# Block products for the last six contraction tiles of a fused decoder layer's first down projection

## What is computed

```python
x = x + 0.5 * swiglu(rmsnorm(x, ffn1_norm), w_gate, w_up, w_down)   # first block, hidden width 2816
u = rmsnorm(x, mix_norm)
proj = u @ w_in                     # convolutions, RG-LRU scan, SSD scan follow
x = x + concat(lru_out, ssd_out) @ w_out
x = x + 0.5 * swiglu(rmsnorm(x, ffn2_norm), ...)                    # second block, same shapes
y = rmsnorm(x, final_norm)
```

## Time and profile before

| | us |
|---|---|
| median of 3 runs (lowest, highest) | 2099.49 (2099.32, 2099.60) |
| the profiled execution | 2098.3 |
| its span, first to last instruction | 2096.6 |
| TensorE busy | 2082.2 |
| DVE busy | 1473.5 |
| POOL busy | 950.2 |
| ACT busy | 865.9 |
| DMA, mean over the span | 109 GB/s |

### The profile page before, as it was taken

One profiled execution on the slowest core, in us unless ns is written; L12 is line 12 of the kernel. 1 busy time (PEld: TensorE's weight loads), 2 busy tenths in 40 slices (PEclk: granted clock), 3 DMA queues, 4 the chain that ended last, 5 costly groups with the idle time before them and its releaser, 6 DMA issues.

```text
span 2096.6 us, 37492 instructions
## 1 busy us (share of the span) xinstructions
PE 2082.2 (99%) x15762; PEld 2051.4 (98%) x15762; DVE 1473.5 (70%) x1361; ACT 865.9 (41%) x1288; POOL 950.2 (45%) x580
## 2 busy tenths in 40 slices
PE   9999999999999999999999999999999999999998
PEld 9999999999999999999999999999999999999998
DVE  7878667676644568878788596786766766675546
ACT  7433333352422235678786540124333333352324
POOL 4644445456643222352534552324544444464650
PEclk9999999999999999999999999999999999999999
DMA  5133232363523322310112422131223222456132
GB/s 174 62 122 122 82 121 102 142 223 122 182 84 106 115 81 101 123 54 32 54 43 75 149 81 94 48 125 61 108 95 109 110 106 88 176 182 226 58 122 81
DMA packets 83383, 227.48 MB, mean 109 GB/s; under 512 B 9608, under 2 KB 18312, under 8 KB 83216
## 3 DMA queue, kind: packets, MB, share of 16 engines
q1 hardware_dynamic: 82064, 224.56, 30.1%
q10 hardware_dynamic: 1152, 0.52, 0.1%
HBM read 162.05 MB, written 63.17 MB: 107 GB/s over the span
## 4 chain that ended last, share of the span: by engine, by line
PE 92%; DVE 3%; ACT 2%; DVEq 1%; issue 1%; DMA 0%; ACTq 0%; POOL 0%; SPq 0%; POOLq 0%
PE banks L997 54%; PE banks L867 28%; PE banks L911 3%; PE banks L1267 2%; PE banks L1178 0%; ACT gate_a L1543 0%; PE banks L1025 0%; PE banks L1032 0%; PE banks L1038 0%; PE banks L1174 0%; PE banks L1156 0%; ACT gate_x L1543 0%; PE banks L1148 0%; DVE decay L2213 0%; DVEq L2178 0%
## 5 line engine op out<-in xcount | busy, mean ns | idle before, releaser
L867 PE MATMUL banks<-u_hi,w_lo 128*128 128x344 f32 x864 | 285.8, 331 | 0.6 <-DVE lru_even L1748 0.3
L867 PE MATMUL banks<-u_hi,w_hi 128*128 128x344 f32 x864 | 275.9, 319 | 0.0
L867 PE MATMUL banks<-u_lo,w_hi 128*128 128x344 f32 x864 | 275.7, 319 | 0.0
L740 POOL TENSOR_TENSOR w_lo<-w_raw,w_hi 128x1024 fp32r<-128x1024 f32 (+1 forms) x68 | 167.1, 2457 | 166.4 <-DVE xbc L2184 123.6
L738 POOL TENSOR_SCALAR w_hi<-w_raw 128x1024 fp32r<-128x1024 f32 (+1 forms) x59 | 67.4, 1142 | 342.3 <-PE banks L867 274.6
L867 PEld LDWEIGHTS banks<-u_hi,w_lo 128*128 128x128 f32 x864 | 162.4, 188 | 7.4 <-issue 4.9
L867 PEld LDWEIGHTS banks<-u_hi,w_hi 128*128 128x128 f32 x864 | 162.4, 188 | 5.1 <-issue 4.3
L867 PEld LDWEIGHTS banks<-u_lo,w_hi 128*128 128x128 f32 x864 | 162.4, 188 | 0.0
L997 PE MATMUL banks<-mix_hi,w_lo 128*128 128x258 f32 x864 | 158.1, 283 | 0.0
L997 PE MATMUL banks<-mix_hi,w_hi 128*128 128x258 f32 x864 | 157.9, 283 | 0.0
L997 PE MATMUL banks<-mix_hi,w 128*128 128x258 f32 x832 | 151.5, 283 | 0.0
(11 more groups left out here) (374 smaller groups left out, 6677.3 us busy)
## 6 DMA issues: line engine op xcount, KB each, us to landing
w_raw<-in_gate_up SPq DMA_DIRECT2D x46, 512.0 KB, 4.1
hidden<-up SPq DMA_DIRECT2D x44, 516.0 KB, 3.6
raw<-in_gate_up SPq DMA_DIRECT2D x40, 512.0 KB, 4.1
w_raw<-in_w_in SPq DMA_DIRECT2D x36, 512.0 KB, 4.1
hidden_mix<-hidden_part SPq DMA_DIRECT2D x16, 1032.0 KB, 4.8
slot_raw<-hidden_mix SPq DMA_DIRECT2D x16, 1032.0 KB, 5.8
slot_raw<-hidden SPq DMA_DIRECT2D x12, 1032.0 KB, 6.8
raw<-in_down SPq DMA_DIRECT2D x16, 512.0 KB, 4.6
```

The costliest lines, as they stand in the source:

```text
L740: pool.tensor_tensor(w_lo[s][:, 0:n], w_raw[s][:, 0:n], w_hi[s][:, 0:n].bitcast(F32), ALU.subtract).then_inc(split, 1)
L867: end = pe.matmul(out[:, c, 0:CH], w[s][:, k * P:(k + 1) * P], x[kx][:, c * CH:(c + 1) * CH], start=(first and n == 0), stop=(last and n = ...
```

## The change

In the first block only, the down groups go on over the six tiles left: `NL` = 28 takes the place of the old count and `NE` = 32 is the new one, with `LAST_K` = 3 contraction tiles in each block of groups 28 to 31, so that a product there is 3 x 2 x 3 = 18 matmuls. The units d1 are gone. Hidden pairs 0, 9 and 10 get mixes too; pair 0 is read back from DRAM for it. Seven *end slots* of 3x516 columns are loaded, and their parts made, at the end of group 27 and in group 28. The preparation of u (high, square, low, total) is put between the products of groups 29 to 31, the rest of it after group 31, and `sums("mix")` stands after the seventh contraction tile of xbc 0. In both blocks `slot_low` of slots 1 to 3 stands one product earlier in group 19, and slot 7 later.

The core of the change, from the file's diff:

```diff
+def depth(q):
+    return 4 if q < NL else LAST_K
...
             def store_hidden(f, i):
...
+            def store_mix(f, n):
+                sp.wait_ge(*f.h_mixed.past(n + 1))
+                sp.dma_start(d.hidden_mix[:, n], f.part_end if n == FT // 2 - 1 else f.part).then_inc(f.mix_stored.sem, 16)
...
             def down(f, x_src, src):
-                tag = f.tag
+                if f is f1:
+                    store_mix(f, MIXED)
                 load_slot(f, 0)
                 for m in range(2):
                     x_again(f, x_src, m)
                 store_hidden(f, NG // 2 - 1)
+                if f is f1:
+                    store_mix(f, MIXED + 1)
                 for m in range(2, 4):
                     x_again(f, x_src, m)
                 down_weights(f, src, NG)
                 for o in range(1, 5):
                     load_slot(f, o)
...
-                    for k in range(4):
+                    for k in range(depth(q)):
...
-                hooks = {0: {6: lambda: sums("mix", m1.tot, KT - 1)}, 3: {3: dt_turn}, 4: {6: bc_turn}, 5: {5: dt_widen}}.get(q)
+                hooks = {0: {7: mix_sums}, 3: {3: dt_turn}, 4: {6: bc_turn}, 5: {5: dt_widen}}.get(q)
...
                 if o == 0:
-                    act.wait_ge(*f.mix_stored.past(16 * MIXED))
+                    act.wait_ge(*f.mix_stored.past(16 * (MIXED + 2 * (f is f1))))
...
+            next_after = {number(NL + 1, "p2"): lambda: two_next(0), number(NL + 2, "p2"): lambda: two_next(2),
+                          number(NE - 1, "p5"): lambda: (next_high(4), next_square(4))}
...
                         if q // 2 <= MIXED:
-                            hidden_mixes(f, q // 2)
+                            hidden_mixes(f, q // 2 - 1, f.u, f.part)
+                        elif f is f1:
+                            hidden_mixes(f, q // 2, f.u, f.part)
...
                     if q == NG - 1:
-                        between = {"p2": lambda: slot_low(f, 0), "p5": lambda: weight_sums(f, NG), "p7": lambda: slot_low(f, 1),
-                                   "p3": lambda: slot_low(f, 2)}
+                        between = {"p2": lambda: slot_low(f, 0), "p5": lambda: (weight_sums(f, NG), slot_low(f, 1)),
+                                   "p7": lambda: slot_low(f, 2), "p3": lambda: slot_low(f, 3)}
                     corners(f, q, between)
                 last_corner(f, NG - 1)
-                slot_low(f, 3)
...
+                def last_product():
+                    product(f, NG // 2, 1)
+                    if f is f1:
+                        dve.drain()
+                        hidden_mixes(f, f.mixes - 1, f.u, f.part_end)
...
+                    hooks.update({NL - 2: {"p6": lambda: slot_low(f, 14)},
+                                  NL - 1: {"p5": lambda: slot_low(f, 15), "p7": lambda: (slot_low(f, 16), weight_sums(f, NL)),
+                                           "p3": lambda: slot_low(f, 17)},
+                                  NL: {"p1": lambda: slot_low(f, 18), "p6": lambda: slot_low(f, 19), "p5": lambda: slot_low(f, 20)},
+                                  NL + 1: {"p5": lambda: next_low(0), "p3": lambda: next_low(1), "p4": lambda: add("mix", 1, m1)},
+                                  NL + 2: {"p5": lambda: next_low(2), "p3": lambda: next_low(3), "p4": lambda: add("mix", 2, m1)},
+                                  NE - 1: {"p1": lambda: add("mix", 3, m1), "p7": lambda: next_low(4),
+                                           "p3": lambda: add("mix", 4, m1)}})
```

More of the change, by code:

```diff
@@ L156, in make_plan @@
             p.unit(("u" + tag, j), gate_up[2 * j + 1], KT)
[L157 to L166, removed]
+    for m in range(KT):
+        p.unit(("d2", m), d.down2[m, :, 8 * BLOCKS * P:], N_LAST)
+    s = 1
     for q in range(XT):
@@ L196, in make_plan @@
     p.before_ffn2 = list(p.taken)
-    ffn("2", 0)
+    s = 0
+    for m in range(WHOLE):
+        p.take(("d2", m), s)
+        s = 1 - s
     return p
@@ L569, in gate_up_groups @@
                         store_hidden(f, q // 2 - 1)
+                        if q > 2:
+                            store_mix(f, q // 2 - 2)
+                    if f is f1 and q == NG - 4:
+                        sp.wait_ge(*f.h_stored.past(32))
+                        for m in range(2):
+                            sp.dma_start(f.again[m], d.hidden[:, 2 * pair_place(0) + m, :]).then_inc(x_landed[m], 16)
             def x_again(f, src, m):
@@ L1234, in tensor @@
             ffn(f2)
+            for m in range(WHOLE):
+                banks_read(f2, ("d2", m))
+                products(("d2", m), f2.hh, f2.hl, ready=f2.hidden.sem if m == 0 else None, base=f2.hidden.base)
             def sum_at(n, here):
@@ new lines, in next_square, with two_next @@
+            def next_square(m):
+                if m == 3:
+                    act.wait_ge(added["mix"], 1)
+                if m == 4:
+                    act.wait_ge(*f1.done.past(number(NE - 1, "p5") + 1))
+                if m >= 6:
+                    act.wait_ge(added["mix"], m - 2)
+                act.activation(m1.c[m][:] if m else m1.tot[:], f1.again[m], ACT.Square).then_inc(squared["mix"], 1)
+            def two_next(m):
+                for k in (m, m + 1):
+                    next_high(k)
+                    next_square(k)
@@ L1692, in scalar @@
             second_pair(f2)
-            groups_and_down(f2, {})
+            groups(f2, {})
+            for t in range(N_LAST):
+                hidden_high(t)
             def piece_square(c, m):
@@ L2331, in vector @@
             norm_turned(f2)
-            groups_and_down(f2, {})
+            groups(f2, {})
+            for t in range(4, N_LAST):
+                hidden_low(t)
+            for m in range(WHOLE):
+                residual(m)
             def piece_residual(c, m):
@@ L2402, in tiles, with down @@
         return w.reshape(-1, P, k * P)
-    def down(w):
-        order = [n * P + r for n in DOWN_ORDER for r in range(P)]
-        return tiles(np.asarray(w)[order])
+    def down(w, order):
+        return tiles(np.asarray(w)[[n * P + r for n in order for r in range(P)]])
     def gate_up(gate, up):
```

367 lines of the change are left out of this document (211 added, 156 removed).

## The result

The changed kernel takes **2106.22 us** (median of 8 runs, 2104.42 to 2106.67), the kernel before on the same chip 2099.51 us (8 runs, 2098.0 to 2100.04). The ratio is 1.0033, with a 95% interval of 1.0024 to 1.0043: slower by 0.33%, where 2094.8 us was forecast and the range ended at 2100.0. The profiled executions say the same: span 2102.7 us against 2096.6 us. (The eight executions of the change lie within 2.3 us, those of one experiment within 4.7, so differences of one or two us between profiled executions are not certain.)

A forecast was written before the change was run, and what follows sets the result against it. TensorE, busy 99% of the span, bounds the kernel; 2098.3 - 7.7 - 2.2 + 4.1 + 0.3 + 0.2 + 0.4 + 0.2 = 2093.6, plus 1.2 for the median: 2094.8 us; range 2090.5 to 2100.0.

The forecast's parts named there:

- The matmuls: Groups 28 to 31: 432 matmuls of units d1 removed, 504 added at 120.0 ns; gain 7.7 us.
- rival spacing of 125 ns: Products of 18 matmuls: spacing 125 ns, gain 5.2 us, time 2097.3; among the small losses, chance 0.30 together.
- The slots' low parts: Start of group 20, both blocks: low parts one product earlier remove waits for `slot_lo`; gain 2.2 of 2.4 us.
- The added mixes, group 19: Before p7 of group 19: mixes delay the DMA burst and slot 1, so TensorE stands 4.1 us.
- upper bound of 6.7: Group 19: stall of 6.7 us if slot 2, issued right behind slot 1, shared the queues equally.
- bound of 3.5: Group 19: stall of 3.5 us if the burst ran at 394 GB/s all through.
- Group 21: Group 21: the last mixes on DVE delay the reading of p7, for which p4 waits; loss 0.3 us.
- Groups 28 to 31: DVE's readings come late for the shorter products: loss 0.2 us in group 28, 0.4 at two later passages.
- With both SBUF instructions free of POOL that ends at 18.5: Groups 29 and 30: p1's reading ends 18.5 to 20.4 us in, due at 19.4; loss 0.2 us a passage.
- DVE becomes the bound: Groups 29 to 31: DVE waits for POOL, TensorE waits 3.4 us a group; 2104 us, chance 0.10.
- Into xbc: Into xbc 0: product chain loses 0; the sum comes 1.4 us later, root ends at 705.6; loss 0.2, at most 1.5.
- more is lost than I count: Several small places: slot 1 later, 125 ns spacing, or 1 us more per end group; 2096 to 2100, chance 0.30.

The follow-up runs named there:

- experiment 4: The kernel before, with only the low parts of slots 1 to 3 one place earlier: 2095.64 us, ratio 0.9988.
- Experiment 1: The changed kernel, with the store of pair 9's mixes behind x_again 2 and 3 and group 20's weights on SP's queue: 2099.27 us, ratio 1.0002.
- experiment 8: experiment 6's kernel, with slot 1's high part one place later on ACT in group 19, between the copies of p6 and p5: 2095.36 us, ratio 0.9981.
- experiment 3: The changed kernel, with adds 1, 2 and 3 of the end groups moved to p1 of group 30 and p1 and p2 of group 31: 2102.68 us.
- experiment 5: The changed kernel with the edits of Experiment 1 and experiment 3 together: 2096.62 us, ratio 0.999.
- experiment 2: The changed kernel, with x_again 2 and 3 issued behind slot 4, the mixes' store left in front of slot 1: 2104.51 us, ratio 1.0025.
- experiment 7: The changed kernel, with ACT's copies of p6 and p5 ahead of slot 1's high part in group 19, low parts as before the change: 2104.94 us.
- experiment 6: experiment 5's kernel, with u tile 4's low part, adds 4 and 5 and tile 5's square earlier in group 31: 2095.99 us, ratio 0.9985.

## Why the prediction was wrong

The forecast was 11 us too low. The places it named were the places of the loss, but four terms were too small: the wait in group 19, TensorE's clock (which had no term), groups 28 to 31, and the way into xbc.

- **The matmuls.** Forecast -7.7, measured -7.2: from group 20 to xbc 0 TensorE takes 230.99 - 0.79 = 230.2 us without its idle time before, 226.42 - 3.41 = 223.0 after. Right within half a microsecond; the rival spacing of 125 ns did not come, for products of 18 start 2.16 us apart (672.38, 674.54 and 676.70 in group 30), 120 ns a matmul.
- **The slots' low parts.** Forecast -2.2, and experiment 4 measured 2.9 between profiled executions and 3.6 between medians. Right, as far as the interval can tell.
- **The added mixes, group 19.** The mechanism was exactly the one forecast: the mixes end at 441.9 (forecast 442.4), the burst waits for them, slot 1 is late, and ACT's copy of p6 stands behind its high part. The size of the burst failed. The step "so the new burst, from 442.4, is through at 452.2" took the bytes and the 9.8 us of the earlier burst of six transfers, but this one's weights came at 452.56 and 453.8, 11.9 us after 441.9, and slot 1, the forecast 2.7 us behind them, at 456.49 instead of 454.8. The other 0.4 us of the 6.24 are TensorE's: it came to p7 at 452.7, not 453.1, since this execution was ahead by about that much from its start. The stretch from 442 to 448 shows where the rate was low:

```profile
442.00:444.00 2.00, 2.00 (x19) 2.00 (x18) 1.91 (x2) 0.00 (x0) 1.24 (x1) 1.00 0.58 225
444.00:446.00 2.00, 2.00 (x19) 2.00 (x18) 1.63 (x3) 1.12 (x2) 0.61 (x1) 1.00 1.01 270
446.00:448.00 2.00, 2.00 (x19) 2.00 (x19) 0.70 (x1) 0.12 (x1) 0.87 (x1) 1.00 1.01 312
448.00:450.00 2.00, 2.00 (x19) 2.00 (x18) 0.16 (x1) 1.80 (x1) 0.00 (x0) 1.00 1.04 395
```

  The DMA engines are busy there (share 1.01), at 270 and 312 GB/s: the store and the loads overlap, and full rate comes only once the store is through (ACT's wait for it ends at 447.88). Experiment 1, whose store was issued at 442.19, has such a stretch too, 251 GB/s at a share of 1.03 from 446 to 448. That a large store does this, rather than something else in those 4 us, is argued and not shown. The upper bound of 6.7 that the prediction kept for this term did hold the 6.24. (Its bound of 3.5 for a burst at 394 GB/s does not come out of its rows: 3.2 MB at that rate take 8.1 us instead of 9.8, which gives 2.4.)
- **TensorE's clock had no term.** The prediction said that a wait of TensorE "is paid in full"; it is paid with more. Behind the 6.24 us the engine ran at 1.2 GHz, 1.4 us lost, and near 770 it ran so again, 1.4 us more. In experiment 1, which took the idle time away, neither is there. But the second came back in experiment 8 without such an idle time, and stayed away in experiment 3 with one of 6.14 us, so only the first belongs to the change for certain.
- **Group 21.** Forecast 0.3, measured 0.22. Right.
- **Groups 28 to 31.** Forecast 0.2 in group 28, where no wait came, and 0.4 at the two passages behind it, where 1.84 + 1.15 were measured. The step "With both SBUF instructions free of POOL that ends at 18.5, with one POOL instruction waited for before each at 20.4. It is due at 19.4." was followed by a choice of 0.2 us, near the free end. In the trace both SBUF instructions of the passage met POOL (1.92 and 2.06 us), and the u low part ahead of it (1.97 us) had already made the reading of p7 0.9 us late, at 658.30: 20.4 + 0.9 - 19.4 = 1.9 us, which is what TensorE waited. The u low part ahead of p7 was in the change and was left out of the sum. That the rest agrees to a tenth is luck: the prediction's own terms add to 18.8, not 18.5, and POOL cost the two instructions 0.63 and 0.83 us, not 0.95 each; the two errors cancel. The rival "DVE becomes the bound" named this mechanism and priced it at 3.4 us a group; the truth lay between. The Trainium skill's rule (SBUF — State Buffer, the section on two separate sides), that such a DVE instruction and a GpSimd instruction reading SBUF exclude each other, agrees with these rows: 1.92 us instead of 1.29.
- **Into xbc.** Forecast 0.2, measured 2.2 of idle time. Two steps failed. "It ends 8.6 to 9.4 us after the last matmul of group 31", where the sums come 9.9 us in: the chain of readings, three u low parts and adds ended 10.9 us after 695.38, at 706.3, since the last reading began 0.9 us after group 31's end, behind a u low part and an add, and POOL's 3.33 us instruction on xbc's weights stood in the way of the first u low parts. And the step "xbc 1 started near 705.5", "now the root ends at 705.6", looked at the root alone; the next wait, of xbc 2 for `conv_in`, hangs on the same root through 19.6 us of VectorE's and ACT's work, and had only 0.7 us of slack (`conv_in` done at 719.94, xbc 2 started at 720.64).

Together: 3.2 us in group 19 with its clock, 3.4 from group 20 to xbc 0, 2.4 in xbc, 1.4 of clock later. The rival "more is lost than I count" had named the queue and the end groups, but it priced one failure at a time (2097, 2097.3), and so the range ended at 2100.0; here they came together.

With the repairs the change gains (2095.4 to 2096.6 us), but one of its parts alone, the earlier low parts, gains as much (2095.6 us). Seven products for eight in the last six tiles took 7 us of matmuls away, and even in the repaired kernel of experiment 5 waits that the wider form didn't have took back 4.4 us of them; where the rest went was not traced.

## What to carry to other kernels

When one wait is put at the head of a DMA queue, look at what stands behind it and who needs that first; here an order of queue entries with the same bytes was worth 7 us. On an engine that is 99% busy, a stall can cost more than its own length: here the half clock behind two of them cost 1.4 and 1.5 us on top. Before a shorter product is put in, add up what the reading engine must do per product, with every instruction that can meet POOL at its longer duration, and follow a chain that starts later than before to its second consumer, not its first.

## What the runs showed of the hardware

- The granted clock was 0.50 after idle times of TensorE of 6.24, 6.14, 3.56 and 2.55 us (the change, and experiments 3, 2 and 7), and stayed at 1.00 after 1.70 us (experiment 8), 1.60 (7), 1.17 (6) and 0.85 us (5). An idle time of 1.83 or 1.84 us at the same place of the program was followed by the half clock in experiments 2 and 7 and by 1.00 in the change and in experiment 1. So a stall of about 2 us has no fixed price.
- The Trainium skill has a rule for this (TensorE: Matmul & The Clock Gate, the section on why this matters for your kernels): long idle gaps between bursts of matmuls send the engine back to half clock. The traces agree on the gaps of 6.24, 6.14 and 3.56 us. Those of 2.55, 1.84 and 1.83 us are shorter than the page's limit, and the clock fell behind them too; there the measurement decides. The prediction had not used the rule.
- The clock also fell where TensorE was busy, near 770, in the change and in experiments 2, 7 and 8 (0.68 in 765 to 770), and not in experiments 1, 3, 5 and 6, where the same part of the program ran at 1.00. Experiment 8 has no idle time of TensorE above 1.8 us anywhere in its trace, so this second fall is not the echo of the first, and the 1.4 us that it cost the change in its profiled execution may be missing in another. What decides it stays open. It may also be there in some executions of the kernel before: of its 33 beside experiments 1 to 4, 16 took 2097.7 to 2098.4 us and 17 took 2099.3 to 2100.2, 1.5 us more, nearly all at a mean granted clock of 0.998 instead of 0.999. No trace of the longer kind was kept.
- Two steps of a queue had nearly the same price: 2.9 and 2.7 us for each 1.06 MB put ahead of a load (experiments 1 and 2 and the change).
- VectorE instructions with two SBUF inputs (128x1032) took 1.92 to 2.07 us beside POOL's of 128x384 and 1.23 to 1.29 us without; POOL's took 2.00 us instead of 1.02.
- Not tried: taking POOL's work out of groups 29 to 31, which would measure the turns of VectorE and POOL by themselves, and the sums of squares one contraction tile earlier.
